# Dense matmuls read their moving operand from the last column to the first, and each stage's operand gets a distance of its own from the weights

## The reference, cut to what matters

```python
u = rms_norm(h, pre_w) * (1 + scale) + shift          # latent and context tokens, from c @ w_ada
z, xbc, dt, qkv, b, a = _split_proj(u @ w_in)         # then convolutions, scans, norms
h_lat = h_lat + gate_l * rms_norm(y @ w_out, post_w)
...
for l in range(2):
    proj = _rmsnorm(x, attn_norm_g[l]) @ w_in[l]      # q, k, v and three conv parts, 6 x 1024
    x = x + jnp.concatenate([attn, conv], axis=-1) @ w_out[l]
    hm = _rmsnorm(x, mlp_norm_g[l]) @ w_up[l]         # 2048 -> 8192
    x = x + jnp.square(jax.nn.relu(hm)) @ w_down[l]
```

## Time and profile before

| | us |
|---|---|
| median of 2 runs | 3028.68 |
| the two runs | 3028.11, 3029.24 |
| the profiled execution | 3026.63 |
| its span, first to last instruction | 3024.8 |
| TensorE busy in the span | 2981.0 |

### The profile page before, as it was taken

One profiled execution on the slowest core, in us unless ns is written; L12 is line 12 of the kernel. 1 busy time (PEld: TensorE's weight loads), 2 busy tenths in 40 slices (PEclk: granted clock), 3 DMA queues, 4 the chain that ended last, 5 costly groups with the idle time before them and its releaser, 6 DMA issues.

```text
span 3024.8 us, 68274 instructions
## 1 busy us (share of the span) xinstructions
PE 2981.0 (99%) x28670; PEld 2823.5 (93%) x28670; DVE 1863.7 (62%) x2510; ACT 1333.8 (44%) x1732; POOL 295.3 (10%) x351
## 2 busy tenths in 40 slices
PE   6999999999999999999999999999999999999999
PEld 2688888888989999999999999999999999999999
DVE  3677777688876666555455555566665555555554
ACT  3455455455454444444343333444444443333333
POOL 0000000000111212110010000211122110000000
PEclk8999999999999999999999999999999999999999
DMA  9612212323955454555555555544545555555554
GB/s 398 276 58 85 85 60 83 122 101 113 394 184 203 180 178 174 190 195 192 191 191 192 193 193 195 222 177 172 180 173 189 192 191 191 191 193 193 195 194 153
DMA packets 82964, 547.13 MB, mean 181 GB/s; under 512 B 9125, under 2 KB 13365, under 8 KB 18928
## 3 DMA queue, kind: packets, MB, share of 16 engines
q1 hardware_dynamic: 78448, 523.27, 47.5%
q10 hardware_dynamic: 2192, 15.40, 1.3%
q0 software_dynamic: 2160, 6.05, 0.6%
HBM read 540.46 MB, written 7.36 MB: 181 GB/s over the span
## 4 chain that ended last, share of the span: by engine, by line
PE 95%; DMA 1%; DVE 1%; ACT 1%; PEld 0%; issue 0%; PEldq 0%; POOL 0%; SPq 0%; ACTq 0%; DVEq 0%; POOLq 0%
PE bank L446 29%; PE bank L447 28%; PE bank L448 28%; PE bank L864 1%; DMA raw<-stream 1%; PE bank L731 1%; PE bank L737 1%; PE bank L967 1%; DMA xr<-x_t 1%; PE bank L773 0%; PE bank L950 0%; PE bank L789 0%; PE bank L975 0%; PE bank L1179 0%; DVE rs L1726 0%
## 5 line engine op out<-in xcount | busy, mean ns | idle before, releaser
L425 ACT CAST w_hi<-raw 128x2048 fp32r<-128x2048 f32 x443 | 846.9, 1912 | 1222.0 <-PE bank L448 1221.9
L430 DVE TENSOR_TENSOR w_lo<-raw,w_hi 128x2048 fp32r<-128x2048 f32 x443 | 1020.1, 2303 | 549.5 <-ACT w_hi L425 549.2
L446 PE MATMUL bank<-a_lo,w_hi 128*128 128x256 f32 (+1 forms) x3568 | 1060.3, 297 | 0.5 <-PEq L459 0.3
L447 PE MATMUL bank<-a_hi,w_lo 128*128 128x256 f32 (+1 forms) x3568 | 1034.9, 290 | 0.0
L448 PE MATMUL bank<-a_hi,w_hi 128*128 128x256 f32 (+1 forms) x3568 | 1034.6, 290 | 0.0
L446 PE MATMUL bank<-h_lo,w_hi 128*128 128x256 f32 x3552 | 990.0, 279 | 3.8 <-DVE h_lo L2136 3.8
L447 PE MATMUL bank<-h_hi,w_lo 128*128 128x256 f32 x3552 | 981.5, 276 | 0.0
L448 PE MATMUL bank<-h_hi,w_hi 128*128 128x256 f32 x3552 | 981.4, 276 | 0.0
L446 PEld LDWEIGHTS bank<-a_lo,w_hi 128*128 128x128 f32 x3568 | 672.2, 188 | 24.6 <-DVE g_X L1906 2.7
L448 PEld LDWEIGHTS bank<-a_hi,w_hi 128*128 128x128 f32 x3568 | 670.1, 188 | 17.1
L447 PEld LDWEIGHTS bank<-a_hi,w_lo 128*128 128x128 f32 x3568 | 671.3, 188 | 12.2
(11 more groups left out here) (360 smaller groups left out, 2273.8 us busy)
## 6 DMA issues: line engine op xcount, KB each, us to landing
raw<-stream SPq DMA_DIRECT2D x485, 1024.0 KB, 4.8
gate_raw<-stream ACTq DMA_DIRECT2D x12, 1024.0 KB, 7.9
xr<-x_t SPq DMA_DIRECT2D x4, 1024.0 KB, 16.3
q_raw<-stream SPq DMA_DIRECT2D x8, 512.0 KB, 9.6
x_res<-x_t SPq DMA_DIRECT2D x1, 2048.0 KB, 16.6
bias_table<-bias SPq DMA_DIRECT2D x1, 2048.0 KB, 11.1
bias<-bias_table ACTq DMA_DIRECT2D x1, 2048.0 KB, 11.2
out_t<-x_res SPq DMA_DIRECT2D x4, 512.0 KB, 5.0
```

The lines of the kernel that those rows point to most:

```text
L425: act.copy(w_hi[u.slot][:], raw[u.raw][:]).then_inc(hi_ready, 1)
L430: dve.tensor_tensor(w_lo[u.slot][:], raw[u.raw][:], w_hi[u.slot][:], ALU.subtract).then_inc(lo_ready, 1)
L446: pe.matmul(acc, wh, lo[:, k, 0:n], start=(k == first), stop=False)
L447: pe.matmul(acc, wl, hi[:, k, 0:n], start=False, stop=False)
```

## The change

1. A helper, `backward`, turns a two-dimensional view around: it begins at the last column and has a step of -1. Every dense product (in `unit_mm` and in lines 789 to 791) takes it for its moving operand and for its PSUM output, so that column t of the operand still goes to column t of the output. The stationary operand is as before.
2. `SKEW` goes. `u`, the mixed heads and hidden quarters of each layer, and the four normed inputs get tiles of their own, which overlap in the same memory, with these offsets in bytes from a multiple of 512: `u` 320; `a` 256 in layer 0 and in the first block's output projection, 384 in layer 1; `h` 288 (attention, layer 0), 352 (feed-forward, layer 0), 416 (attention, layer 1), 224 (feed-forward, layer 1).
3. `w_spare` now lies at a multiple of 512 bytes, like the other weight halves. `cs`, a small tile, moves to the end of the memory.

The sequence of instructions on each engine and their waits are the same as before. The core of the diff:

```diff
-SKEW = 48
+U_SKEW = 320
+A_SKEW = (256, 384)
+H_SKEW = (288, 352, 416, 224)
...
-        top["at"] += 4 * SKEW
-        a_hi = put("a_hi", KT * T, F32R)
-        a_lo = put("a_lo", KT * T, F32R)
-        cs = put("cs", 2 * KT)
-        top["at"] += 4 * (P - SKEW - 2 * KT)
+        A0 = top["at"]
+        u_hi, u_lo = (put(n, KT * T, F32R, at=A0 + U_SKEW + 4 * KT * T * k) for k, n in enumerate(("u_hi", "u_lo")))
+        a_hi, a_lo = ([put(n, KT * T, F32R, at=A0 + skew + 4 * KT * T * k) for skew in A_SKEW] for k, n in enumerate(("a_hi", "a_lo")))
+        top["at"] += 4 * (P + 2 * KT * T)
+        cs = put("cs", 2 * KT, at=4 * (53200 - T - HALF - 2 * KT))
...
-        h_hi = put("h_hi", KT * L, F32R)
-        h_lo = put("h_lo", KT * L, F32R)
+        H0 = shared - 192
+        h_hi, h_lo = ([put(n, KT * L, F32R, at=H0 + max(skew, 192 + (skew - 192) % 512) + 4 * KT * L * k) for skew in H_SKEW]
+                      for k, n in enumerate(("h_hi", "h_lo")))
+        top["at"] += 4 * 2 * KT * L + max((skew - 192) % 512 for skew in H_SKEW)
...
-            w.append(put(f"w_spare{g}", D, F32R, at=4 * (RAW * D + 2 * SPL * D + SKEW + KT * T + KT * L + g * D)))
+            w.append(put(f"w_spare{g}", D, F32R, at=X_RES - 4 * (2 - g) * D))
...
+        def backward(x):
+
+            (step, rows), (one, n) = x.ap
+            return bass.AP(x.tensor, x.offset + (n - 1) * one, [[step, rows], [-one, n]])
...
-            acc = psum[u.bank][:, 0:n]
+            acc = backward(psum[u.bank][:, 0:n])
...
-                pe.matmul(acc, wh, lo[:, k, 0:n], start=(k == first), stop=False)
-                pe.matmul(acc, wl, hi[:, k, 0:n], start=False, stop=False)
-                last = pe.matmul(acc, wh, hi[:, k, 0:n], start=False, stop=(k == final))
+                xl, xh = backward(lo[:, k, 0:n]), backward(hi[:, k, 0:n])
+                pe.matmul(acc, wh, xl, start=(k == first), stop=False)
+                pe.matmul(acc, wl, xh, start=False, stop=False)
+                last = pe.matmul(acc, wh, xh, start=False, stop=(k == final))
...
+                (h_hi3, h_lo3), (m_hi3, m_lo3), (y_hi3, y_lo3) = normed3(2 * l), normed3(2 * l + 1), mixed3(l)
```

More of the change, by code:

```diff
@@ L354, in build @@
         top["at"] = shared
-        h_hi = put("h_hi", KT * L, F32R)
-        h_lo = put("h_lo", KT * L, F32R)
+        H0 = shared - 192
+        h_hi, h_lo = ([put(n, KT * L, F32R, at=H0 + max(skew, 192 + (skew - 192) % 512) + 4 * KT * L * k) for skew in H_SKEW]
+                      for k, n in enumerate(("h_hi", "h_lo")))
+        top["at"] += 4 * 2 * KT * L + max((skew - 192) % 512 for skew in H_SKEW)
         mo = put("mo", KT * L, at=shared + 4 * KT * L)
-        bias = put("bias", 2 * HEADS * L, at=4 * (RAW * D + 2 * SPL * D + SKEW + KT * L))
+        bias = [put("bias", 2 * HEADS * L, at=A0 + skew + 4 * KT * L) for skew in A_SKEW]
         n_sq, n_acc, n_ln, n_rs = (put(n, L) for n in ("n_sq", "n_acc", "n_ln", "n_rs"))
@@ L361, in build @@
         small = put("small", 64)
-        gate_raw = [put(f"gate_raw{k}", D, at=4 * (RAW * D + 2 * SPL * D + SKEW + KT * T + KT * L + k * D)) for k in range(2)]
+        gate_raw = [put(f"gate_raw{k}", D, at=X_RES - 4 * (2 - k) * D) for k in range(2)]
         for w, g in ((w_hi, 0), (w_lo, 1)):
-            w.append(put(f"w_spare{g}", D, F32R, at=4 * (RAW * D + 2 * SPL * D + SKEW + KT * T + KT * L + g * D)))
+            w.append(put(f"w_spare{g}", D, F32R, at=X_RES - 4 * (2 - g) * D))
         gate_acc = put("gate_acc", 3 * 512, at=top["at"])
@@ L445, in unit_mm, with mixed3, normed3 @@
                 wh, wl = (w[u.slot][:, k * P:(k + 1) * P] for w in (w_hi, w_lo))
-                pe.matmul(acc, wh, lo[:, k, 0:n], start=(k == first), stop=False)
-                pe.matmul(acc, wl, hi[:, k, 0:n], start=False, stop=False)
-                last = pe.matmul(acc, wh, hi[:, k, 0:n], start=False, stop=(k == final))
+                xl, xh = backward(lo[:, k, 0:n]), backward(hi[:, k, 0:n])
+                pe.matmul(acc, wh, xl, start=(k == first), stop=False)
+                pe.matmul(acc, wl, xh, start=False, stop=False)
+                last = pe.matmul(acc, wh, xh, start=False, stop=(k == final))
             if part[1] == KT:
                 last.then_inc(unit_done, 1)
-        u_hi3, u_lo3 = (a[:].rearrange("p (k t) -> p k t", t=T) for a in (a_hi, a_lo))
-        y_hi3, y_lo3 = (a[:, 0:KT * L].rearrange("p (k t) -> p k t", t=L) for a in (a_hi, a_lo))
-        h_hi3, h_lo3 = (a[:].rearrange("p (k t) -> p k t", t=L) for a in (h_hi, h_lo))
+        u_hi3, u_lo3 = (a[:].rearrange("p (k t) -> p k t", t=T) for a in (u_hi, u_lo))
+        def mixed3(l):
+            return (a[l][:, 0:KT * L].rearrange("p (k t) -> p k t", t=L) for a in (a_hi, a_lo))
+        def normed3(m):
+            return (a[m][:].rearrange("p (k t) -> p k t", t=L) for a in (h_hi, h_lo))
         def leave(eng, k):
@@ L494, in diagonals @@
             n = 2 * (h1 - h0)
-            return (d3(bias[:, 2 * L * h0:2 * L * h1], L),
+            return (d3(bias[0][:, 2 * L * h0:2 * L * h1], L),
                     bass.AP(scratch[1].tensor, P - 1, [[PERIOD - 1, P], [P * PERIOD, n], [1, L]]))
@@ L788, in quarter @@
                     wh, wl = (w[slot][:, (j * 4 + i) * P:(j * 4 + i + 1) * P] for w in (w_hi, w_lo))
-                    pe.matmul(acc, wh, u_lo3[:, k, 0:n], start=(k == 0), stop=False)
-                    pe.matmul(acc, wl, u_hi3[:, k, 0:n], start=False, stop=False)
-                    last = pe.matmul(acc, wh, u_hi3[:, k, 0:n], start=False, stop=(k == KT - 1))
+                    xl, xh = backward(u_lo3[:, k, 0:n]), backward(u_hi3[:, k, 0:n])
+                    pe.matmul(acc, wh, xl, start=(k == 0), stop=False)
+                    pe.matmul(acc, wl, xh, start=False, stop=False)
+                    last = pe.matmul(acc, wh, xh, start=False, stop=(k == KT - 1))
                 if i1 == 4 and m == QUARTERS - 1:
@@ L1071, in _ @@
             mixed_order = [*range(8, KT), *range(8)]
+            y_hi3, y_lo3 = mixed3(0)
             quarters = (S["y_ready"], {8: 1, 12: 2, 0: 3, 4: 4, 5: 5, 6: 6, 7: 7})
@@ L1110, in first_normed @@
             def first_normed(u, e, second=None):
+                h_hi3, h_lo3 = normed3(e - 1)
                 ready = (S["h_ready2"], {k: (e - 1) * KT + k + 1 for k in range(KT)})
@@ L1577, in weighted_hi @@
                 tile = ds(i * (4 * L) + j * L, L)
-                act.mul(h_hi[:, tile], x_res[:, tile], par(name, i * 4 + (l * KT + j))).then_inc(S["h_hi_ready"], 1)
+                act.mul(h_hi[m][:, tile], x_res[:, tile], par(name, i * 4 + (l * KT + j))).then_inc(S["h_hi_ready"], 1)
             norm_root(0)
@@ L1597, in _ @@
                 if l:
-                    act.dma_start(bias[:], scratch[1]).then_inc(S["bias_ready"], 16)
+                    act.dma_start(bias[l][:], scratch[1]).then_inc(S["bias_ready"], 16)
                 def at(i, j, n=1, k=1):
@@ L1675, in turn_ @@
                             tile = i * (4 * L) + ((q % 2) * KT + j) * L
-                            act.copy(a_hi[:, ds(tile, L)], hbuf[:, (2 + j % 2) * L:(3 + j % 2) * L]).then_inc(S["hi_relu"], 1)
+                            act.copy(a_hi[l][:, ds(tile, L)], hbuf[:, (2 + j % 2) * L:(3 + j % 2) * L]).then_inc(S["hi_relu"], 1)
                         elif not isinstance(i, int) or u.c + i * 4 + 2 < N_SEQ:
@@ L2135, in weighted_lo @@
                 tile = ds(i * (4 * L) + j * L, L)
-                stt(h_lo[:, tile], x_res[:, tile], par(name, i * 4 + (l * KT + j)), h_hi[:, tile], ALU.mult, ALU.subtract
+                stt(h_lo[m][:, tile], x_res[:, tile], par(name, i * 4 + (l * KT + j)), h_hi[m][:, tile], ALU.mult, ALU.subtract
                     ).then_inc(S["h_ready2"], 1)
@@ L2275, in turn_ @@
                             tile = ds(i * (4 * L) + ((q % 2) * KT + j) * L, L)
-                            tt(a_lo[:, tile], hbuf[:, (2 + j % 2) * L:(3 + j % 2) * L], a_hi[:, tile], ALU.subtract
+                            tt(a_lo[l][:, tile], hbuf[:, (2 + j % 2) * L:(3 + j % 2) * L], a_hi[l][:, tile], ALU.subtract
                                ).then_inc(S["mlp_ready"], 1)
```

24 lines of the change are left out of this document (12 added, 12 removed).

## The result

The changed kernel takes 3115.05 us (median of 2 runs, 3114.31 to 3115.78) against 3028.68: a ratio of 1.0288, 95% interval 1.0271 to 1.0305. It is slower by 86 us. The profiled execution has a span of 3112.5 us, 87.7 more than before.

A forecast was written before the change was run, and what follows sets the result against it. TensorE bounds the kernel: product count times start-to-start interval. Span 3024.8 us plus 11.2 for more products at 118.1 ns gives 3036.0; with 1.8 and 2.1 us beyond the span, 3039.9, say 3040 us; range 2950 to 3140.

The forecast's parts named there:

- 12,000 products in the earlier trace keep it to the nanosecond: Large stages: 113.3 ns per 256-column product taken as a level that stays, through both a and h.
- I take a quarter at the upper level: 256-column products after the change: 5,100 at 118.1 ns, 2,330 more than before, +11.2 us.
- The 14% before: Share of 256-column products at the upper level before the change: 2,770 of 20,400, spare ones included.
- no new distance is zero: Operand to weight halves: seven new distances of 224 to 416 bytes, none zero; spare halves leave zero, the slowest, too.
- rival two: Products of lines 446 to 448: backward stream meets the weight load at every distance; +123 us, 3152 us; chance 0.21.
- the forecast's own range: Whole kernel: 2990 (all at 113.3 ns, shorter loads) to 3085 us (three quarters at 118.1 ns).
- within 2%: Whole kernel: the forecast outcome, levels stay and the mix shifts, about 3040 us; chance 0.55.
- slower by over 2%: Whole kernel: the outcome if rival two or Rival three holds; chance 0.29.
- 420 products or fewer in 50 us: Large stages: count that would show rival two, with 192 ns for all three loads; 444 before.
- Rival three: Moving read or PSUM write: negative step handles one column instead of two; 234 ns interval, +2462 us; chance 0.08.
- Rival one: 256-column products: interval falls below 113.3 ns; half of 6.7 ns gives 2960 us, the whole 2892; chance 0.16.
- the level goes with the number of loads held up: Weight loads: interval level follows how many of three loads are held up by some 4.5 ns.

The follow-up runs named there:

- e1: The changed kernel with its seven distances, but moving operand and PSUM output read and written forward again: 3121.11 us, ratio 1.0302.
- e7: The changed kernel read and written forward, u at 160, a at 64 and 320, h at 320, 256, 384 and 448 bytes: 3094.42 us.
- e2: The kernel before with its 192 bytes, but moving operand and PSUM output both backward: 3113.07 us, ratio 1.0272.
- e3: The kernel before with only the moving operand read backward, the PSUM output written forward: 3112.85 us.
- e4: The kernel before with only the PSUM output written backward, the moving operand read forward: 3026.20 us.
- e9: The changed kernel's layout, forward, u at 320 and all else at 192 bytes: median 3020.31 us of 12 runs, ratio 0.9995.
- e10: The changed kernel's layout, forward, u at 320 and all else at 448 bytes: 3020.88 us of 10 runs, ratio 0.9992.
- e6: The changed kernel, forward, u at 448, a at 128 and 160, h at 448, 480, 192 and 320 bytes: 3092.62 us.
- e5: The changed kernel read and written forward, with all seven distances at 192 bytes: 3024.08 us (12 runs), ratio 1.0000.

## Why the prediction was right or wrong

Right: what bounds the kernel, and that the time is the count of products times the interval. The rise of 87.7 us is all there. Right too that nothing beside the products would pay, and that no instruction, wait or transfer would show.

Wrong: the argument that "12,000 products in the earlier trace rows keep it to the nanosecond", so that the level "looks more like a fixed length of load and handover". It does look so, but in the feed-forward parts only one distance in eight has it, and only read forward. The step that failed is "I take a quarter at the upper level". After the change it is all of them in the large stages, at 117.8, 118.3 or 120.0 ns. With 87.7 / 20,400 = 4.3 ns per product on average that term is 87.7 us instead of 11.2. The 14% before was worked out rightly from the earlier trace rows; the quarter had no row behind it. Nor does it help that no new distance is zero: 256 is zero modulo 256, and forward it has the 120 ns of zero (e1, e7). I had written that in the rows "the distance 192 is the good one and no new distance is known", and gave that the smaller chance. With two levels on view and one distance for the good one, the honest reading was that leaving it goes to the other level.

So 3115 us is inside the stated 2950 to 3140 only because that was drawn to take in most of rival two. It is outside the forecast's own range of 2990 to 3085, and "within 2%", with 0.55, did not come true, where slower by over 2% had 0.29. (The 3085 is a span; with the 3.9 us that the prediction adds elsewhere it would be 3089.)

Rival two came true in kind: slower, in every large stage, past the 3.4 ns it named as its turning point. Its price was too high, 6.7 ns for all, where most stages took 4.5 to 5. Of its signs, 420 products or fewer in 50 us came in one kind of stage (419 with `a` at 384, 425 to 427 in the others), and loads of 192 ns did not come. Of its mechanism, "a backward stream meets the weight load in every product", the runs show that reading backward costs (e2, e3), but not that this is a meeting with the load; and the distances alone would have done it too (e1).

Rival three is excluded at 192 bytes, by e4 for the write and by e2 for the read: if a backward column cost more in itself, twice the columns would cost twice as much more. But the 512-column products are 233.5 ns apart in e2 and 233.3 in the kernel before, while the 256-column ones went from 113.3 to 117.8. (At 320 bytes the wide ones do differ, 230.3 ns forward in e1 and 233.6 backward; the 256-column ones there, 117.8 and 120.0.)

Rival one (below 113.3 ns) was met nowhere for 256 columns, in thirteen kernels. For 512 columns a distance of 320 gives 230.3 ns forward, 3 ns less.

Wrong as well: that the level goes with the number of loads held up. I named the test myself, and it failed: in the changed kernel the interval moved with all loads at 187 to 188 ns. For forward reads it fails too. It tells the two levels at 192 and 448 apart (e9, e10), but e6's stage with `h` at 320, forward and at 117.8 ns, has no load held up. These are the loads of `w_hi`, and those of `w_lo` took 187 ns:

```profile
L458 PEld LDWEIGHTS bank<-h_hi,w_hi x340: 188/188/188, 2409.9 to 2529.7; 128*128 128x128 f32 x170
L456 PEld LDWEIGHTS bank<-h_lo,w_hi x340: 187/188/188, 2410.1 to 2529.8; 128*128 128x128 f32 x170
```

The matmuls' own durations are longer in the slow stages. In the changed kernel, with `h` at 352 and `a` at 384:

```profile
L457 PE MATMUL bank<-h_hi,w_lo x482: 282/282/282, 1269.8 to 1439.8; 128*128 128x256 f32 x161
L458 PE MATMUL bank<-h_hi,w_hi x482: 279/279/279, 1269.9 to 1439.9; 128*128 128x256 f32 x161
```

```profile
L457 PE MATMUL bank<-a_hi,w_lo x473: 282/284/284, 2929.8 to 3099.7; 128*128 128x256 f32 x158
```

They were 276 in the large stages before. But they were 281 in the forward stage of the earlier trace rows as well, and ends of matmuls are modelled, so this does not tell which of the two reads gives way. What in the engine makes the levels is open.

## What to carry to other kernels

In a stream of float32r products as short as their weight loads, the place of the moving operand relative to the weights was worth 3.5 to 6% of the interval here: try it in steps of 32 bytes over 256, in forward order, and give each stage of one execution another distance, so that one profile reads several. Then look at more than one execution and more than one kind of stage, since a distance may have a second level that lasts a whole stage. If it does, look at what broke the stream just before. A level that is constant over thousands of products is not thereby a floor or a safe place: ask what else was held constant.

## What the runs showed of the hardware that I had not expected

- The interval of a 256-column product with a 128-column load beside it is 113.3, 117.2 to 118.7 or 120.0 ns, by the distance modulo 256 bytes (in steps of 32), by the direction of the read and by how the stream was entered. The Trainium skill (TensorE: Matmul & The Clock Gate, section Step-by-step: what each phase is for) says that TensorE reads the moving operand and the weights through two independent ports. In time these runs show them not to be independent: e5 and e1 differ in the operands' distances from the weights alone, and they are 97 us apart.
- At the same distance the direction of the moving read can decide the level (113.3 and 117.8 ns at 192 bytes, e3); the direction of the PSUM write does not (e4, 3026.20 us).
- The same instructions at the same addresses run at 113.3 or 117.8 ns through nearly a whole feed-forward part, and which it is settles at a break of 0.67 us in the stream (e9).
